# Two-model transformer step on one Trainium2 core: modulation vectors dealt out anew, gates inside last steps, fifth sums moved forward

## The reference

```python
mod = (jax.nn.silu(c) @ ada_w[layer] + ada_b[layer]).reshape(B, 3, 3, D)
h = modulate_pre(x, g[0, 0], mod[:, 0, 0], mod[:, 0, 1])     # shift and scale, before a layer
y = swiglu_ffn(h, ffn_w_in[layer, 0], ffn_w_out[layer, 0])
x = gated_post_add(x, y, g[0, 1], mod[:, 0, 2], 0.5)         # gate, behind it
...
mod = (cond_lat @ ada_w[i] + ada_b[i])[:, None, :]           # second block: 6 vectors a layer,
modc = (cond_ctx @ ada_w[i] + ada_b[i])[None, None, :]       # for the tokens and for the context
```

## Time and profile before

| | |
|---|---|
| median of 3 runs | 2338.65 us (2333.1 to 2341.84) |
| the profiled execution | 2337.85 us, span 2335.8 us |
| PE busy | 2168.5 us, 93% of the span |
| DVE, ACT busy | 1291.9 us (55%), 931.4 us (40%) |
| DMA | 411.42 MB, mean 176 GB/s |
| mean granted PE clock | 0.952 |

### The profile page before, as it was taken

How to read it: one execution, slowest core, us unless ns; L and a number is a source line. 1 busy time by engine, 2 the same in 40 slices (tenths; PEclk the granted TensorE clock), 3 DMA queues, 4 the chain that set the end, 5 groups by cost and what they waited for, 6 DMA issues and landing times.

```text
span 2335.8 us, 34631 instructions
## 1 busy us (share of the span) xinstructions
PE 2168.5 (93%) x14014; PEld 1889.1 (81%) x14014; DVE 1291.9 (55%) x2057; ACT 931.4 (40%) x1376; POOL 103.9 (4%) x156
## 2 busy tenths in 40 slices
PE   4999897999889998998998998898999999898999
PEld 2998786998789987667997997576878778777997
DVE  2677656767727665545445754864222233855454
ACT  2334424334523345435345543653222132554343
POOL 2000000000100000000001000002000000200000
PEclk7999898999869998988999999899999999999999
DMA  8797695887548764753554221023443523215553
GB/s 292 247 311 261 218 319 184 278 292 281 165 149 278 274 224 147 253 180 127 181 180 153 91 91 54 1 91 122 149 142 127 198 77 112 88 40 198 173 172 124
DMA packets 246604, 411.42 MB, mean 176 GB/s; under 512 B 10221, under 2 KB 191942, under 8 KB 246470
## 3 DMA queue, kind: packets, MB, share of 16 engines
q1 hardware_dynamic: 246470, 409.54, 50.7%
HBM read 408.47 MB, written 1.05 MB: 175 GB/s over the span
## 4 chain that ended last, share of the span: by engine, by line
PE 82%; DVE 8%; DMA 4%; ACT 3%; POOL 2%; issue 2%; SPq 0%; DVEq 0%; ACTq 0%; POOLq 0%
PE bank L1789 20%; PE bank L1737 14%; PE bank L1738 14%; PE bank L1739 14%; DMA ada<-in_ada_w 3%; PE bank L1854 3%; PE bank L1704 3%; PE bank L1855 3%; PE bank L1856 3%; PE bank L1888 1%; PE bank L1723 1%; DVE w_lo L1104 1%; PE bank L1757 1%; DVE astat L1501 1%; PE bank L1975 1%
## 5 line engine op out<-in xcount | busy, mean ns | idle before, releaser
L1104 DVE TENSOR_TENSOR w_lo<-stage,w_hi 128x2048 fp32r<-128x2048 f32 x255 | 585.4, 2298 | 580.5 <-ACT w_hi L719 579.9
L1737 PE MATMUL bank<-h_hi,w_hi 128*128 128x256 f32 (+1 forms) x2432 | 741.2, 305 | 25.1 <-POOL h_lo L671 18.6
L719 ACT CAST w_hi<-stage 128x2048 fp32r<-128x2048 f32 x255 | 485.1, 1904 | 635.9 <-PE bank L1739 250.7
L1738 PE MATMUL bank<-h_lo,w_hi 128*128 128x256 f32 (+1 forms) x2432 | 734.7, 302 | 0.0
L1739 PE MATMUL bank<-h_hi,w_lo 128*128 128x256 f32 (+1 forms) x2432 | 734.1, 302 | 0.0
L1737 PEld LDWEIGHTS bank<-h_hi,w_hi 128*128 128x128 f32 x2432 | 474.3, 195 | 56.2 <-issue 39.8
L1738 PEld LDWEIGHTS bank<-h_lo,w_hi 128*128 128x128 f32 x2432 | 474.5, 195 | 14.8 <-issue 1.2
L1739 PEld LDWEIGHTS bank<-h_hi,w_lo 128*128 128x128 f32 x2432 | 473.9, 195 | 14.1
L1789 PE MATMUL bank<-w_hi,h_hi 128*128 128x512 f32 x776 | 246.1, 395 | 10.4 <-DVE h_lo L1113 9.2
L1789 PE MATMUL bank<-w_lo,h_hi 128*128 128x512 f32 x776 | 244.2, 392 | 0.0
L1789 PE MATMUL bank<-w_hi,h_lo 128*128 128x512 f32 x776 | 243.9, 392 | 0.0
(11 more groups left out here) (210 smaller groups left out, 1970.5 us busy)
## 6 DMA issues: line engine op xcount, KB each, us to landing
ada<-in_ada_w SPq DMA_DIRECT2D x120, 1024.0 KB, 5.5
stage<-in_ffn_w_in SPq DMA_DIRECT2D x88, 1024.0 KB, 7.5
stage<-in_ffn_w_out SPq DMA_DIRECT2D x44, 1024.0 KB, 4.9
stage<-in_ffn_w_gu SPq DMA_DIRECT2D x44, 1024.0 KB, 5.1
stage<-in_ffn_w_down SPq DMA_DIRECT2D x22, 1024.0 KB, 4.8
stage<-in_a_w_in SPq DMA_DIRECT2D x12, 1024.0 KB, 9.5
stage<-in_diff_w_in SPq DMA_DIRECT2D x12, 1024.0 KB, 5.0
ada<-in_kv_ada_w SPq DMA_DIRECT2D x8, 1024.0 KB, 7.1
```

The source lines that it names most:

```text
L719: a.copy(w_hi[:, s, :], stage[:, s, :]).then_inc(hi_done, 1)
L1104: v.tensor_tensor(w_lo[:, s, :], stage[:, s, :], w_hi[:, s, :].bitcast(F32), ALU.subtract).then_inc(lo_done, 1)
L1737: m.matmul(dst[:, 0:T], wh, h_hi[:, h0:h0 + T], start=(k == ks[0]), stop=False)
L1738: m.matmul(dst[:, 0:T], wh, h_lo[:, h0:h0 + T], start=False, stop=False)
```

## The change

The vectors are dealt out anew: the stages now make 5, 2, 5, 0, 5, 8, 3, 0, 1, 0 and 1. `dv` is set for stage 6 too. `VECS` gives the order in which they are made, `mv` finds the place of a stage's own vector in it, and all four readers of a vector go through it. The halves of the sparse attention stand in J = 1, 2, 3, 5, 6, 7, 9, 10, 11, 13, 14, 15, 17, 18, 19 and 21, its sums before the values of a job and in another bank. The gates of feed-forward 8 go into its step 10 and those of the convolution into its step 3 (after part 1), the latter in banks 4 and 5. The fifth sum goes from the last product of the second tile to the last product of the first. `down` loses the variant that made a vector in its first step.

```diff
-CMP_AT = 16
+CMP_AT = 14
+VECS = [*range(9), 11, 12, 13, 9, 10, *range(14, 27), 28, 29, 30, 27, 31]
...
+        def mv(s, j):
+
+            return VECS.index(s["v0"] + j)
+
+        def bias_col(p):
+
+            v = VECS[p]
...
-                     ks=[3, 4, 5, 6, 7, 0, 1, 2] if kind == "diff" else list(range(KC)), w_in=w_in, w_out=w_out, T=T, v=N["vec"], nvec=nvec, v0=v0, dv=len(subs) in (0, 2, 4), u=N["unit"], c=N["chunk"],
+                     ks=[3, 4, 5, 6, 7, 0, 1, 2] if kind == "diff" else list(range(KC)), w_in=w_in, w_out=w_out, T=T, v=N["vec"], nvec=nvec, v0=v0, dv=len(subs) in (0, 2, 4, 6), u=N["unit"], c=N["chunk"],
...
-        add("conv", io["a_w_in"][0], io["a_w_out"][0], 256, 4, 3, norm_col(0, 1, 0), norm_col(0, 1, 1), one, 4, 3, 4)
+        add("conv", io["a_w_in"][0], io["a_w_out"][0], 256, 2, 3, norm_col(0, 1, 0), norm_col(0, 1, 1), one, 4, 3, 4)
-        add("ffn", io["ffn_w_in"][1, 0], io["ffn_w_out"][1, 0], 256, 4, 11, norm_col(1, 0, 0), norm_col(1, 0, 1), half, 11, 2, 11)
-        add("nsa", io["b_w_in"][0], io["b_w_out"][0], 256, 6, 14, norm_col(1, 1, 0), norm_col(1, 1, 1), one, 5, 1, 4)
-        add("ffn", io["ffn_w_in"][1, 1], io["ffn_w_out"][1, 1], 256, 0, 17, norm_col(1, 2, 0), norm_col(1, 2, 1), half, 11, 2, 11)
+        add("ffn", io["ffn_w_in"][1, 0], io["ffn_w_out"][1, 0], 256, 5, 11, norm_col(1, 0, 0), norm_col(1, 0, 1), half, 11, 2, 11)
+        add("nsa", io["b_w_in"][0], io["b_w_out"][0], 256, 8, 14, norm_col(1, 1, 0), norm_col(1, 1, 1), one, 5, 1, 4)
+        add("ffn", io["ffn_w_in"][1, 1], io["ffn_w_out"][1, 1], 256, 3, 17, norm_col(1, 2, 0), norm_col(1, 2, 1), half, 11, 2, 11)
-        add("ffn", io["ffn_w_gu_2"][0], io["ffn_w_down_2"][0], 512, 5, 23, col_at["norm2_g_2"], None, one, 11, 2, 11)
+        add("ffn", io["ffn_w_gu_2"][0], io["ffn_w_down_2"][0], 512, 1, 23, col_at["norm2_g_2"], None, one, 11, 2, 11)
...
-        nsa_vec = {2 + 2 * n: (n // 2, n % 2) for n in range(12)}
+        nsa_vec = {1 + 4 * n // 3: (n // 2, n % 2) for n in range(16)}
...
-            return bank[h if s["kind"] in ("nsa", "gqa") else 6 + h]
+            return bank[h if s["kind"] in ("nsa", "gqa") else 4 + h if s["kind"] == "conv" else 6 + h]
...
+                    halves = {2: (0, 0), 3: (0, 1), 6: (1, 0), 9: (1, 1)}
+                    for n in range(12):
+                        load_unit(u, col_unit(s["w_in"], (1, 2, 0)[n % 3] * D + n // 3 * WCOL), KC)
+                        u += 1
+                        if n in halves:
+                            vi, half = halves[n]
+                            load_vec(s["v"] + vi, *ada_src(s["v"] + vi), half)
...
+                        if j == 10 and T == 512:
+                            gate(s, tag, 1)
...
-                        if j == 10 and T == 256:
+                        if j == 10:
                             gate(s, tag, 0)
-                            mid_split(s, 0)
+                            if T == 256:
+                                mid_split(s, 0)
                         step(j)
-                        if s["dv"]:
-                            if j == 9:
-                                acc_col(s["v"] + 2, 5)
+                        if s["dv"] and j == 9:
+                            acc_col(s["v"] + 2, 5)
+                        if s["nvec"] == 5:
                             acc_ops(s["v"] + 3, range(0, 4) if j == 9 else range(4, 6))
-                        elif s["nvec"] == 5:
-                            vec_row(s["v"] + j - 6)
-                            vec_col(s["v"] + j - 6)
-                    if T == 512:
-                        gate(s, tag, 0)
-                        gate(s, tag, 1)
...
+                        if j == 1:
+                            vec_col(s["v"])
                         if j == 3:
+                            vec_col(s["v"] + 1)
                             gate(s, tag, 0)
+                            mid_split(s, 0)
...
-                        vec_row(s["v"] + j)
-                        vec_col(s["v"] + j)
-                    mid_split(s, 0)
+                        if j in (0, 2):
+                            vec_row(s["v"] + j // 2)
...
-                        if last and s["dv"] and s["nvec"] == 5:
+                        if tt == 0 and j == nb - 1 and s["dv"] and s["nvec"] == 5:
...
+                        if s["kind"] == "conv" and j == 0 and tt == 1:
+                            pe.wait_ge(mid_done, s["c"] + 8)
...
-                    if J - 1 in nsa_vec and nsa_vec[J - 1][1]:
-                        vec_sum(s["v"] + nsa_vec[J - 1][0], z=7)
                     if J in nsa_vec:
                         vi, half = s["v"] + nsa_vec[J][0], nsa_vec[J][1]
-                        if not half:
-                            pe.wait_ge(ada_col, rv(vi - 1) + 1)
+                        if not half and vi > s["v"]:
+                            pe.wait_ge(ada_rowed, rowed(rv(vi - 1)))
...
+                        if J - 1 in nsa_vec and nsa_vec[J - 1][1]:
+                            vec_sum(s["v"] + nsa_vec[J - 1][0], z=6, o=256)
...
                     up_step(9, None, 2, (0, 2), False, {(0, 1): (lambda: acc_sum(s["v"] + 2, 5),)} if s["dv"] else None)
-                    if own:
-                        vec_acc(v9, 1)
-                        also[0, 1] = (lambda: vec_sum(v9), lambda: vec_acc(v10, 0))
-                    if early:
+                    if T == 256:
                         also[1, 0] = (lambda: gate(s, tag, 0),)
+                    else:
+                        also[0, 1] = (lambda: gate(s, tag, 0),)
+                        also[1, 0] = (lambda: gate(s, tag, 1),)
                     up_step(10, None, 2, (0, 2), False, also)
...
-                    for j in range(4):
-                        if j:
-                            up_step(j, None, 3, (0, 2, 6), False, {(0, 1): (lambda: vec_sum(s["v"] + j - 1),),
-                                                                   (1, 0): (lambda: vec_acc(s["v"] + j, 0),)})
-                        else:
-                            up_step(j, None, 3, (0, 2, 6), True)
-                        vec_acc(s["v"] + j, 1)
-                    vec_sum(s["v"] + 3)
-                    pe.wait_ge(mid_done, c + 8)
+                    v0, v1 = s["v"], s["v"] + 1
+
+                    def early_gate():
+
+                        pe.wait_ge(ada_col, rv(v1) + 1)
+                        gate(s, tag, 0)
+                    up_step(0, None, 3, (0, 2, 6), True)
+                    vec_acc(v0, 1)
+                    up_step(1, None, 3, (0, 2, 6), False, {(0, 1): (lambda: vec_sum(v0),)})
+                    vec_acc(v1, 0)
+                    up_step(2, None, 3, (0, 2, 6), False)
+                    vec_acc(v1, 1)
+                    up_step(3, None, 3, (0, 2, 6), False, {(0, 1): (lambda: vec_sum(v1),), (1, 1): (early_gate,)})
```

More of the change, by code:

```diff
@@ L527, in _ @@
             cmp_late = []
-            late = []
-            def single_vec(v):
-                for w in late:
-                    load_vec(w, *ada_src(w), 1)
-                late.clear()
-                if v is not None:
-                    load_vec(v, *ada_src(v), 0)
-                    late.append(v)
             def load_tables(s):
@@ L1352, in nsa_dve @@
                         dve.wait_ge(pe_s, t.at((tag, "pv", i)))
+                        if J - 2 in nsa_vec and nsa_vec[J - 2][1]:
+                            vec_col(s["v"] + nsa_vec[J - 2][0], z=6, o=256)
                         if br == 1:
@@ L1679, in turn_over @@
                             acc_col(s["v"] + 3, 2)
[L1680 removed]
+                        if j in last_acc:
                             acc_ops(s["v"] + 4, last_acc[j])
@@ L1757, in gate, with down @@
                     t.done(m.matmul(gate_bank(s, h)[:, :], ones[:, :], diag[:, h, :], start=True, stop=True), pe_s, (tag, "gate", c, h))
-            def down(s, tag, vec, after, after_s):
+            def down(s, tag, after, after_s):
                 T = s["Td"]
@@ L1822, in down @@
                         step(j, None)
-                        if j == 2:
+                        if j == 2 and s["nvec"] == 5:
                             pe.wait_ge(mid_done, s["c"] + 2 * nb)
@@ L2124, in up_step @@
                                     f()
-                early = s["kind"] == "ffn" and T == 256
                 if s["kind"] == "ffn":
@@ L2173, in _ @@
                     wide_pe(s, tag)
-                if s["kind"] in ("ffn", "conv") and not early:
-                    for k in range(s["Td"] // 256):
-                        gate(s, tag, k)
                 nxt = subs[si + 1] if si + 1 < len(subs) else None
@@ L2183, in after @@
                         turn(nxt, tt - 2)
-                down(s, tag, s["v"] + 4 if early and s["nvec"] == 5 and not s["dv"] else None, after, nxt)
+                down(s, tag, after, nxt)
                 if nxt:
```

70 lines of the change are left out of this document (21 added, 49 removed).

## The result

The changed kernel takes 2370.26 us (median of 4 runs, 2368.99 to 2370.69), the kernel before 2335.99 in four runs (2333.1 to 2341.84): a ratio of 1.0134, 95% interval 1.0114 to 1.0154. It is slower by 1.3%, outside the range of the prediction. The span went from 2335.8 to 2368.3 us, the mean granted clock from 0.952 to 0.937.

The account below looks back on a forecast made before the run. The prediction took PE's work plus its waits at turns as the bound. From 2337.85 us, -22.9 - 11.7 - 3.5 + 3.7 + 3 + 5.1 + 22 = -4.3 gave 2334 us, range 2318 to 2350.

Parts of the forecast that it names:

- Fifteen intervals are 108 us: Sparse attention: sixteen halves at a mean interval of 7.2 us, paced by piece landings with two slots.
- the term of 2 us for the clock: Sparse attention: 2 us added for clock lost behind waits.
- The prediction's +22: Sparse attention: 22 us longer (+9 to +46), 20 from the intervals and job steps, 2 for clock.
- -22.9: Feed-forward 8: 22.9 us shorter, since four vectors leave and the gates move into step 10.
- the place of the gates: Feed-forward 8: gates inside step 10 at 1.72 us each at most; the end goes from 13.34 to 6.0 us.
- -11.7: Convolution: 11.7 us shorter (-20 to -8), with a new 5.5 us stall ahead of its gate.
- The wait ahead of each fifth sum: Feed-forwards with a fifth vector: PE waits 2.0 us for DVE, as the sum comes 5.5 us earlier.
- +5.1: Feed-forward 6: three sums of 1.7 us on PE; DVE's 31 us of added work hides.
- +3 (0 to 5): Three fifth sums: 3 us in all for lower-clock stretches behind their stalls.
- B, the ring keeps up: Sparse attention: four more halves cost only +9.1 us, the whole 2321 us; chance 0.18.
- C, the ring paces every half: Sparse attention: intervals of 7.8 to 9.0 us cost +31 to +46, the whole 2343 to 2358 us; chance 0.17.
- F, the clock: Sparse attention: waits ahead of all halves keep PE at the lower clock, up to 70 us more, about 2400; chance 0.02.

Follow-up runs that it names:

- experiments 5 to 7: Attention pieces an eighth of their size in the changed kernel, in Experiment 4's kernel and in c4_n6_spaced: attention 199.7, 200.4 and 178.2 us.
- c4_n6_spaced: Changed kernel with four vectors in the convolution, its gate after the last step, six in the attention, a half every second step: 2323.62 us, ratio 0.993.
- Experiment 4: c4_n6_spaced with the attention's twelve halves standing three in four steps: 2374.89 us, attention 235.8 us.
- experiment 9: Changed kernel with feed-forward 8's two gates back behind its last step: 250.4 us up to `down` in place of 246.0, the whole 2370.47 us.
- experiment 8: Changed kernel with the fifth sum twelve matmuls later and the convolution's gate diagonal made ahead of the split: 2350.03 us.
- d6_tiny: Experiment 4's kernel with the attention's pieces an eighth of their size: attention 200.4 us in place of 235.8.
- best1: c4_n6_spaced with the fifth sum twelve matmuls later: 2321.46 us, ratio 0.9933.

## Why the prediction was wrong

**The step that failed** is "Fifteen intervals are 108 us ... and 2 for clock lost behind waits", and in it above all the term of 2 us for the clock, which measured 30.5. The first and the last half start here:

```profile
927.80 3.63 PE L1703 MATMUL bank<-ada,cond 128*32 128x512 f32 x16
...
1069.92 2.55 PE L1703 MATMUL bank<-ada,cond 128*32 128x512 f32 x16
```

That is 142.1 us for fifteen intervals, 9.47 each in place of 7.2, and 34 us over. By its terms the stage grew by 56.8 us like this: 8.2 of full-speed work, 18.1 of idle time, and 30.5 for the clock. The prediction's +22 has 9.1 for work (four halves and two sums), 2 for the clock and what is left, 10.9, for waits. So the clock was 28.5 too low and the waits 7.2, the work 0.9 too high: together the 35 us of the miss.

- *The waits.* Those of PE for pieces I had right in kind: 20.9 us at eleven places, where there had been 6.1 at five. The landings are those of before, 5.5 us from issue in the median and up to 8.1.
- *The clock.* This is the larger part. The time at the lower clock went from 41 to 108 us. I had put 2 us on it, and gave the rival of the clock 0.02, since the stretch of before had a mean of 0.94 in spite of five waits. Three of those five were 1 us or less, and the one of 2.08 was followed by a half at the upper level; I took a mean over few waits for a rule about many. That rival's price, up to 70 us, was too high, for the clock came back between.
- *The tail.* When all halves are done at J = 21, the jobs behind them stand alone. From there to `down` are 23.6 us at a clock of 0.78 (1071.9 to 1095.5), before 11.3 at 0.80; from the last half's start the changed kernel took 4.8 us more than I had reckoned with job steps at 2.87 us. In the other orders of experiments 5 to 7 this part is larger.

Experiments tell how the 57 us hang together. The changed kernel's pieces made small took away 41 us (241.0 to 199.7), half of them idle time and half clock, so that 41 us hang on the pieces being full-size, that is on the waits. This edit takes traffic away with the waits; that traffic alone is not the cause is said by `c4_n6_spaced`, with the most of it and a clock of 0.91. The 15 that stay over the kernel before are 8 of work and 10 of clock, less 3 of idle time. Experiment 4 shows that the same twelve halves, dense, cost 52 us more than spaced, so that density and not number makes waits and clock.

The Trainium skill, "TensorE: Matmul & The Clock Gate", section "HAM oscillation", says that bursts of matmuls between waits for transfers begin at the lower level. The trace agrees in part: behind five of the eleven waits the half ran at the lower level (1.93 to 1.94 us for 1.07), behind five at the upper; the page's own case has longer waits and the lower level after every one. At spacing 2 the lower clock held 30 to 45 us of the stage. The Trainium skill, "DMA: Bandwidth & Descriptors", section Bandwidth, by whose 358 GB/s the ring would have kept up (the prediction's estimate), did not help. At 229 GB/s in the stretch, well below that figure, the pieces still came late: a slot is loaded only after it is used, and a landing took 4.9 to 8.1 us from there.

**What held.** In feed-forward 8 the sum gave -22.9, measured -24.2, and the place of the gates gave 4.4 of it (experiment 9, about 4 expected); the wait ahead of `down` was 2.49 for 2.6. In the convolution -11.7 against -12.7: the stall stood where DVE's order put it, 5.59 us for 5.5, and went with that order (experiment 8); from there to `down` 15.4 for 15.9. The wait ahead of each fifth sum was 2.06 for 2.0, and from `down` to the key/value stage's first product 9.4 for 9.5. The three sums of feed-forward 6 cost +4.2 with the stage behind it for +5.1.

**Mis-sized.** The term "+3 (0 to 5)" for the clock behind the three fifth sums. After the first two the lower clock lasted 6.8 us each, after the third 3.4, 8.5 us of time in all, so that these three stretches came to +1.6, +0.8 and +7.0 rather than near -1.4, -0.1 and +4.7: 6 us together.

**The rivals.** B, the ring keeps up, is refuted by the eleven waits. C, the ring paces every half, came nearest with intervals of 7.8 to 9.0 and a bound of 2358; the measured 9.47 lies beyond it, since C too reckoned the work at the upper level. F, the clock, at 0.02, had named the mechanism that made most of the miss, at a price of up to 70 us where 30 were measured.

## What to carry to other kernels

Where work fills holes between small matmuls and itself waits for a ring of two slots, count its spacing against a piece's landing and its use. Here a half in every second step (8.5 us) cost little, and three in four steps cost the waits and about as much again in clock (21 and 21 us in the changed kernel). Spacings between these two were tried only once, with pairs still in adjacent steps, so where the limit lies is open. Where a stage has no idle time, moving work out of it returned its full price (24.2 us for 22.9, the gates' new place among it), but the price where it goes to must be read with that stage's clock, and a stage whose end is left bare may pay too (22 us for twelve halves in experiments 5 to 7). A prerequisite in another engine's list (the diagonal behind a split, a sum 2 us ahead of its last addend) is found by reading that list, and was mended there at no cost seen.

## What the runs showed of the hardware that I had not expected

- Dense halves without waits keep the granted clock at 0.87 to 0.90, and the attention's jobs alone, behind them, have 0.61 to 0.68 (the three kernels with tiny pieces); one stretch of 23.90 us is at 0.50 throughout although PE is busy for 22.84 of it by the profile (`d6_tiny`, 1014.8 to 1038.7).
- Eight matmuls ran at the upper level (1.06 us) directly behind a wait of 2.87 us, and at the lower (1.94) behind one of 1.12 that followed another of 1.85 by little.
- The same attention code took 183.2, 188.7 and 183.3 us in three kernels, and 237.1 to 241.0 in three others, with 30 to 45 and 101 to 108 us at the lower clock. The same shows between runs of one kernel: the ten of `best1` go from 2317.54 us at a mean clock of 0.955 to 2330.08 at 0.947.
